# Sums of squares of keys and queries: one float32 product, or two rounded products of a split

## The reference, cut to what matters

```
gdn_qkv = silu(causal_dwconv(gdn_qkv, gdn_conv_w))
g_q, g_k, g_v = split into 4 heads of 128
def l2_normalize(t):
    return t * rsqrt(sum(t * t, axis=-1) + 1e-6)
g_q = l2_normalize(g_q) * 128 ** -0.5
g_k = l2_normalize(g_k)
```

## Time and profile before

| what | value |
|---|---|
| median of 3 runs | 1473.73 us (1473.54 to 1474.15) |
| the profiled execution | 1472.97 us, of which the span from first to last instruction is 1471.2 us |
| TensorE busy | 1462.1 us, 99% of the span |
| VectorE busy | 954.6 us, 65% |
| ScalarE busy | 820.2 us, 56% |
| GpSimd busy | 215.8 us, 15% |
| granted TensorE clock | 0.999 of full speed |
| HBM traffic | 180 GB/s over the span |

### The profile page before, as it was taken

How to read it: one execution, slowest core, us unless ns; L and a number is a source line. 1 busy time by engine, 2 the same in 40 slices (tenths; PEclk the granted TensorE clock), 3 DMA queues, 4 the chain that set the end, 5 groups by cost and what they waited for, 6 DMA issues and landing times.

```text
span 1471.2 us, 29387 instructions
## 1 busy us (share of the span) xinstructions
PE 1462.1 (99%) x12785; PEld 1414.8 (96%) x12785; DVE 954.6 (65%) x1388; ACT 820.2 (56%) x1264; POOL 215.8 (15%) x126
## 2 busy tenths in 40 slices
PE   9999999999999999999999999999999999999998
PEld 9999999999999989999999999999989999999997
DVE  6655377786655475655558685655478767677766
ACT  6554377655544365544476655554475675555762
POOL 1000143113000261000332040000430001400001
PEclk9999999999999999999999999999999999999999
DMA  9655464227555466555553156555555344553341
GB/s 383 245 195 186 165 229 144 98 107 263 184 196 201 163 218 228 199 186 191 199 177 140 68 197 220 190 201 194 179 215 201 115 144 166 208 191 137 133 155 58
DMA packets 40239, 267.43 MB, mean 182 GB/s; under 512 B 4464, under 2 KB 4976, under 8 KB 10032
## 3 DMA queue, kind: packets, MB, share of 16 engines
q1 hardware_dynamic: 38592, 260.39, 49.6%
q0 software_dynamic: 944, 4.38, 0.7%
q10 hardware_dynamic: 576, 0.79, 0.1%
HBM read 264.49 MB, written 1.05 MB: 180 GB/s over the span
## 4 chain that ended last, share of the span: by engine, by line
PE 97%; DVE 1%; DMA 1%; SPq 0%; ACT 0%; issue 0%
PE PS L600 19%; PE PS L601 19%; PE PS L602 19%; PE PS L594 6%; PE PS L596 6%; PE PS L595 6%; PE PS L636 4%; PE PS L634 4%; PE PS L633 4%; PE PS L674 1%; PE PS L1318 1%; PE PS L1042 1%; PE PS L1336 1%; DMA raw<-in_weights 1%; PE PS L1328 1%; PE PS L1349 1%
## 5 line engine op out<-in xcount | busy, mean ns | idle before, releaser
L600 PE MATMUL PS<-xTH,WH 128*128 128x256 f32 x2256 | 637.6, 283 | 0.1
L602 PE MATMUL PS<-xTH,rawL 128*128 128x256 f32 x2256 | 624.4, 277 | 0.0
L601 PE MATMUL PS<-xTL,WH 128*128 128x256 f32 x2256 | 624.3, 277 | 0.0
L2058 DVE TENSOR_TENSOR rawL<-raw,WH 128x1024 fp32r<-128x1024 f32 (+1 forms) x407 | 495.0, 1243 | 105.9 <-ACT WH L1485 104.9
L1485 ACT ACTIVATE WH<-raw 128x1024 fp32r<-128x1024 f32 (+2 forms) x477 | 484.6, 1047 | 134.7 <-PE PS L636 98.0
L600 PEld LDWEIGHTS PS<-xTH,WH 128*128 128x128 f32 x2256 | 423.9, 188 | 8.1 <-issue 5.3
L601 PEld LDWEIGHTS PS<-xTL,WH 128*128 128x128 f32 x2256 | 423.8, 188 | 2.7 <-issue 1.9
L602 PEld LDWEIGHTS PS<-xTH,rawL 128*128 128x128 f32 x2256 | 424.2, 188 | 0.0
L2755 POOL TENSOR_TENSOR rawL<-raw,WH 128x1024 fp32r<-128x1024 f32 (+3 forms) x71 | 166.5, 2371 | 767.6 <-ACT WH L1485 767.6
L1565 ACT ACTIVATE sg<-PS 128x256 f32<-128x256 f32 x79 | 30.3, 383 | 167.6 <-PE PS L602 167.6
L633 PE MATMUL PS<-WH,hTH 128*128 128x256 f32 x512 | 122.4, 276 | 0.0
(11 more groups left out here) (421 smaller groups left out, 2180.9 us busy)
## 6 DMA issues: line engine op xcount, KB each, us to landing
raw<-in_weights SPq DMA_DIRECT2D x232, 1024.0 KB, 4.8
gb<-in_lngb SPq DMA_DIRECT2D x16, 512.0 KB, 5.7
raw<-in_weights SPq DMA_DIRECT2D x2, 1056.0 KB, 4.8
raw<-in_weights SPq DMA_DIRECT2D x4, 512.0 KB, 5.7
gb<-in_ln SPq DMA_DIRECT2D x4, 512.0 KB, 5.2
cst<-in_consts POOLq DMA_DIRECT2D x1, 1378.5 KB, 9.9
raw<-in_weights SPq DMA_DIRECT2D x4, 256.0 KB, 4.9
xt<-in_x POOLq DMA_DIRECT2D x1, 1024.0 KB, 17.7
```

What stands on the lines that cost most here:

```text
L600: e.matmul(out, u.H(i, c0, 128), xH, start=first, stop=False)
L601: e.matmul(out, u.H(i, c0, 128), xL, start=False, stop=False)
L602: return e.matmul(out, u.L(i, c0, 128), xH, start=False, stop=end)
L2058: e.tensor_tensor(u.L(i, 0, w), u.R(i, w), u.H(i, 0, w).bitcast(F32), ALU.subtract).then_inc(*low_dve.up(k))
```

## The change

The float32 product of the squares with ones is replaced by two fp32r products that add into the same bank: of the squares rounded to fp32r, and of the remainders. ScalarE's Square now writes the rounded squares (`sqH`) straight away. VectorE makes the float32 squares once more (`sqw = v * v`), waits for ScalarE, and subtracts (`sqL = sqw - sqH`). VectorE also copies the ones to an fp32r tile once per layer. On TensorE the square of k 1 is moved two quarters later, and the square of q 1 one quarter later. The scratch tiles lie at places that later tiles (T, U, Z) use.

```diff
+        m.sqH = [put("sqHa", [128, 512], 12, F32R), put("sqHb", [128, 512], 14, F32R)]
+        m.sqw = [put("sqwa", [128, 512], 44), put("sqwb", [128, 512], 46)]
+        m.sqL = [put("sqLa", [128, 512], 44, F32R), put("sqLb", [128, 512], 46, F32R)]
+        m.onesF = put("onesF", [128, 128], 48, F32R)
...
             def squares(nm, i, b):
                 B(("squares", l, nm, i), b, (norm_scale, (l, nm, i, "ln")))
-                e.wait_ge(*conv_act.at((l, nm, i, "sq")))
-                e.matmul(PS[:, b, :], ones, sq[i][:, :], start=True, stop=True).then_inc(*squares_summed.up((l, nm, i)))
+                e.wait_ge(*squares_low.at((l, nm, i)))
+                e.matmul(PS[:, b, :], m.onesF[:, :], m.sqH[i][:, :], start=True, stop=False)
+                e.matmul(PS[:, b, :], m.onesF[:, :], m.sqL[i][:, :], start=False, stop=True).then_inc(*squares_summed.up((l, nm, i)))
...
             quarter("q", 0, 3)
-            squares("k", 1, 4)
             quarter("q", 1, 0)
             quarter("q", 1, 1)
+            squares("k", 1, 4)
             quarter("q", 1, 2)
...
             quarter("v", 0, 3)
+            quarter("v", 1, 0)
             squares("q", 1, 6)
-            for q in range(4):
+            for q in range(1, 4):
                 quarter("v", 1, q)
...
-                e.activation(m.sq[i][:, :].rearrange("p (j s) -> p j s", j=2), dst, ACT.Square).then_inc(*conv_act.up((l, nm, i, "sq")))
+                e.activation(m.sqH[i][:, :].rearrange("p (j s) -> p j s", j=2), dst, ACT.Square).then_inc(*conv_act.up((l, nm, i, "sq")))
...
+            def square_low(nm, i):
+
+                v = kq[:, 2 * i:2 * i + 2, "kq".index(nm), :]
+                e.wait_ge(*conv_act.at((l, nm, i)))
+                if nm == "q":
+                    e.wait_ge(*squares_summed.at((l, "k", i)))
+                link(e.tensor_tensor(m.sqw[i][:, :].rearrange("p (j s) -> p j s", j=2), v, v, ALU.mult))
+                e.wait_ge(*conv_act.at((l, nm, i, "sq")))
+                linked()
+                e.tensor_tensor(m.sqL[i][:, :], m.sqw[i][:, :], m.sqH[i][:, :].bitcast(F32), ALU.subtract).then_inc(*squares_low.up((l, nm, i)))
...
             conv("k", 0)
+            e.tensor_copy(m.onesF[:, :], ones)
             lows("k", 1, 0)
             lows("k", 1, 2)
+            square_low("k", 0)
             conv("k", 1)
             lows("q", 0, 0)
             lows("q", 0, 2)
+            square_low("k", 1)
             conv("q", 0)
             lows("q", 1, 0)
             lows("q", 1, 2)
+            square_low("q", 0)
             conv("q", 1)
             lows("v", 0, 0)
+            square_low("q", 1)
             unit_norm("k", 0)
```

More of the change, by code:

```diff
@@ L365, in program @@
     masks, level_masked = signal("masks"), signal("level_masked")
-    squares_summed, norm_scale, unit_length = [signal(n) for n in ("squares_summed", "norm_scale", "unit_length")]
+    squares_low, squares_summed, norm_scale, unit_length = [
+        signal(n) for n in ("squares_low", "squares_summed", "norm_scale", "unit_length")]
     gram_product, gram_masked, tokens_turned, tokens_scaled = [
@@ L459, in mix_buffers @@
         m.cv = [put("cva", [128, 2, S], 8), put("cvb", [128, 2, S], 10)]
-        m.sq = [put("sqa", [128, 512], 12), put("sqb", [128, 512], 14)]
+        m.sqH = [put("sqHa", [128, 512], 12, F32R), put("sqHb", [128, 512], 14, F32R)]
+        m.sqw = [put("sqwa", [128, 512], 44), put("sqwb", [128, 512], 46)]
+        m.sqL = [put("sqLa", [128, 512], 44, F32R), put("sqLb", [128, 512], 46, F32R)]
+        m.onesF = put("onesF", [128, 128], 48, F32R)
         m.rs = [put("rsa", [128, 512], 16), put("rsb", [128, 512], 61)]
@@ L898, in mix @@
             s = ring[0]
-            kq, cv, sq, U, T, Z, Bs, Eu, wq, ez, zb = m.kq, m.cv, m.sq, m.U, m.T, m.Z, m.Bs, m.Eu, m.wq, m.ez, m.zb
+            kq, cv, U, T, Z, Bs, Eu, wq, ez, zb = m.kq, m.cv, m.U, m.T, m.Z, m.Bs, m.Eu, m.wq, m.ez, m.zb
             def A(key, off, *freed_by):
```

## The result

The changed kernel takes 1482.11 us (median of 6 runs, 1481.09 to 1483.40), the kernel before 1473.94 (6 runs): ratio 1.0057, 95% interval 1.0047 to 1.0067. By that ratio it is 8.4 us slower; the two medians lie 8.2 apart. The forecast was 1481.3.

What follows compares the result with a forecast made beforehand. Prediction: TensorE, busy 99%, bounds the kernel, with the ScalarE and VectorE chain about 0.4 us behind. Layers +3.8 and +3.5 and the copy +0.3 give +7.6 on 1473.73, 1481.3 us; range 1475.8 to 1483.2.

Steps and rivals of the forecast that it cites:

- Rounded matmuls at 0.23 each: TensorE's squares: two rounded matmuls, 0.46 us, replace a float32 one of 0.87, saving 3.2 us over two layers.
- A faster TensorE alone gains no more than the chain's margins: Level mask: an earlier TensorE gains at most about 0.4 us there; the rival, 3.2 us saved whole, had 0.02.
- VectorE and GpSimd take turns for instructions with two SBUF operands, and GpSimd goes ahead of the product: VectorE's pair: main case, 0.60, 1480 to 1482.5 us; rivals VectorE first 0.20, no contention 0.12.
- the upper bound: VectorE's copy of the ones: order GpSimd, VectorE, GpSimd ends 0.27 us later, 0.5 for two layers; forecast took 0.25.
- The first wait 2.8 us: First square, k 0, both layers: TensorE waits 2.8 us for VectorE's subtraction.
- The last square's wait of 1.4 us in the first layer: Square of q 1, first layer: TensorE wants it at 237.2, pair ends at 238.5, stall 1.4 us.
- 0.25 for the square of k 1: Square of k 1, first layer: TensorE wants it at 226.4 and stalls 0.25 us.
- The clock stays at 1.0: TensorE's granted clock in the changed profile: forecast to stay at 1.0, no fall.
- the walk: Step-by-step timing of the engines around the squares in each layer, giving +3.8 us in the first, +3.5 in the second.
- The last scaling 4.2 us late: Last query scaling, first layer: ends at 244.7 instead of 240.5, 4.2 us late.
- the level mask 3.8 and 3.5: Level mask on TensorE: chain's delay less the 0.4 margin, +3.8 us in the first layer, +3.5 in the second.
- The sum: Whole kernel: 3.8 + 3.5 + 0.3 = +7.6 us, with TensorE's saved 3.2 swallowed by waits; median 1481.3.

Runs made afterwards that it cites:

- Experiment 9: Changed kernel, GpSimd's remainders waiting for the pairs, VectorE's and ScalarE's lists reordered to shorten the chain: 1473.57 us; with float32 product of rounded squares 1475.81.
- experiment 1: Kernel before with two rounded products of the rounded squares on TensorE, no remainders of squares on VectorE, ones copied on ScalarE: 1472.16 us, ratio 0.9994.
- experiment 4: Changed kernel with the copy of the ones on ScalarE instead of VectorE: 1480.45 us, ratio 1.0049.
- experiment 7: Changed kernel, all instructions kept, copy ahead of the taps of k 0, GpSimd's four weight remainders per mixer waiting for VectorE's subtractions: 1473.62 us, ratio 0.9995.
- experiment 5: Changed kernel with GpSimd's four weight remainders in each mixer given to VectorE: 1476.44 us, ratio 1.0023.
- experiment 8: ScalarE's Ln and Exp of q 1 put ahead of a weight rounding, VectorE's scaling likewise: changed kernel 1480.90 us (1.0052), kernel before 1473.03 us (1.0001).
- experiment 2: Changed kernel with TensorE's squares of k 0 three quarters later and k 1 two later, VectorE's list unchanged: 1481.90 us, ratio 1.0058.
- experiment 6: Changed kernel with VectorE's pair for k 0 ahead of two weight remainders, later remainders behind the next unit's taps: 1477.48 us, ratio 1.0028.
- experiment 10: The shortened-chain kernel with rounded products, GpSimd's fourth remainder given to VectorE, VectorE's remainders v 1 and z 0 behind T and Eu: 1475.90 us, ratio 1.0020.

## Why the prediction was right, step by step

- **Rounded matmuls at 0.23 each: right.** 228.08 - 227.84 = 0.24 and 228.31 - 228.08 = 0.23. Experiment 9 shows what that is worth when the chain is shorter: 2.2 of 3.2 us.
- **A faster TensorE alone gains no more than the chain's margins: right.** 0.9 us of 3.2, with an interval that reaches to none (experiment 1).
- **VectorE and GpSimd take turns for instructions with two SBUF operands, and GpSimd goes ahead of the product: right.** 2.84 us for the product in the changed kernel, 2.89 and 2.65 for the pair without the copy (experiment 4). Moving GpSimd's turns alone brings the time back to that of the kernel before (experiment 7); taking them away while adding 9.1 us of VectorE's work brings back 5 us (experiment 5). This is shown, not argued.
- **The copy: the upper bound was the true one.** The order was GpSimd, VectorE, GpSimd; so it was the product, not the subtraction, that had the long wait, and the subtraction for k 0 ended at 221.44 + 0.62 = 222.06, where the upper bound gave 221.79 + 0.27. I had taken the middle, 0.25 in all. The level masks of experiment 4 put the copy at 0.35 and 0.33 us, 0.7 in all, a little above even the upper bound of 0.5.
- **The first wait 2.8 us: right in place, 3.0 in size,** by the copy.
- **The last square's wait of 1.4 us in the first layer, and 0.25 for the square of k 1: wrong.** Neither is among the waits, because TensorE came late itself, by the clock. The changed kernel of experiment 8 shows it: in its first layer the clock did not fall behind the same 3.0 us wait, and there TensorE waited for the last square:

```profile
PE PS L989 <- DVE sqLb L2304: 1.2, 1, 1.2
```

- **"The clock stays at 1.0": wrong.** It was at 1.2 GHz for some 3.4 us behind each 3 us wait. That it cost next to nothing is luck: the 1.6 us of TensorE took the place of waits for the chain that the walk had further on (the second layer of experiment 2 is as long without it). In experiment 6, with the chain earlier, TensorE is last behind such a fall.
- **The last scaling 4.2 us late, the level mask 3.8 and 3.5: right in mechanism, a little small.** Measured 4.5, and 4.22 and 3.84. Most of the difference is the copy's 0.27 to 0.35 a layer.
- **The sum.** 8.1 us is accounted for at the two level masks against 7.6 forecast. The last 0.4 us between the two profiled spans comes from stretches of weight matmuls that are no part of the change (last section): 0.6 us gained ahead of the squares, 1.1 lost behind the second mask.

## What to carry to other kernels

When one engine is busy 99% and the others 65%, price an added instruction by the chain behind it and by the order in which other engines get their turns, not by its length: here 11 us of added VectorE work cost nothing once GpSimd's four instructions a layer waited for it, and 8.4 us when they didn't. Where two engines share a port, look at who is waiting when the first of a pair ends: in experiment 4 GpSimd's waiting instruction went ahead both of a product that stood right behind another instruction and of a subtraction that waited for its own engine's result. And work taken off the busiest engine comes back only as far as the next chain's margin, so read that margin first; each wait removed in experiments 9 and 10 uncovered another within some 10 us.

## What the runs showed of the hardware that was not expected

- A copy of 128 elements between float32 and fp32r tiles in SBUF, one operand only, waited for GpSimd too: 0.79 us, ending 0.07 behind GpSimd's Eu at 214.44. In experiment 7, with GpSimd idle, the same copy took 0.23:

```profile
208.90 0.23 DVE L2342 CAST onesF<-cst 128x128 fp32r<-128x128 f32 x1
```

  The Trainium skill, VectorE: DVE Perf Modes, section on mode 2x_2P, says that a `tensor_copy` within SBUF can use both read ports for its one tensor; the trace agrees, in that the copy waited.
- After a wait of 3.0 us TensorE went on at full clock from 221.59 to about 222.7, and was then granted 1.2 GHz for 3.4 us. The length of the wait alone doesn't tell whether the clock falls. It fell behind 1.9 us (experiment 2, first layer), 2.3 us (experiment 6, first layer), 2.1 us (experiment 10, second layer) and 3.0 us, and stayed at 2.4 GHz behind 1.6 and 1.7 us (second layers of experiments 2 and 6), 2.1 us (experiment 10, first layer) and once behind 3.0 us (experiment 8, changed kernel, first layer). Each fall lasted 3.4 us. What decides it stays open.
- The same weight matmuls start 0.1136 us apart for most of a run and 0.1177 in stretches of about 16 or 33 us, and which stretches differs between executions and kernels. The first line is the kernel before, with 122 matmuls in 14 us, the second the changed one, with 126 (the first number in brackets counts them):

```profile
20.00:34.00 14.00, 14.00 (x122) 14.00 (x120) 11.59 (x14) 9.42 (x12) 2.50 (x4) 1.00 1.01 415
```

```profile
20.00:34.00 14.00, 14.00 (x126) 14.00 (x126) 11.65 (x14) 9.46 (x12) 2.50 (x4) 1.00 1.01 415
```

  The clock is 1.00 in both. That is where the 0.62 us ahead of the squares came from; the changed kernel has two such stretches behind the second mask (at 1099 and 1292 us), which cost it 1.1 us. It is a measure of what two single profiles can differ by. Its cause stays open.
